# Products with 256 moving tokens: the order of the high and low products over two column blocks, four k-tiles and two PSUM banks

## The chip, the cores and the metric

The kernel runs on one core of a Trainium2 chip. The time is that of one execution on the device, in microseconds (us); shown are the median of three runs and one profiled execution.

## The reference

Two transformer-like blocks are applied to one sequence of 256 tokens with 2048 channels, all in float32.

```python
def reference(x, c, ctx, ...):
    x = first_block(x, c, ctx, ...)      # 2 layers: adaLN, attention + pooling + Fourier branches, gate, w_out
    return second_block(x, ...)          # 1 layer: gated spatial mixing + LRU, w_out, then an FFN

# first_block, per layer: h is the normed, scaled and shifted x
q, k, v, up, uf, g = split_proj(h @ w_in[l])
out = (mixed * jax.nn.silu(g)) @ w_out[l]
...
# second_block
p = jnp.einsum('bsd,de->bse', h, w_in[l])
x = x + jnp.einsum('bse,ed->bsd', y, w_out[l])
up = jnp.einsum('bsd,df->bsf', h, ffn_w_up[l])
x = x + jnp.einsum('bsf,fd->bsd', jax.nn.gelu(gate) * val, ffn_w_down[l])
```

Nearly all of the arithmetic is in these matrix products. In layer 0 of the first block they run over the 256 tokens and 256 context tokens together, from layer 1 on over the 256 tokens alone.

## The kernel before, in words

**Three products for one.** TensorE multiplies in a reduced float32 form (fp32r), so each operand is split in a high part (rounded) and a low part (the rest). A product of weights W and activations H is made of three: W high x H high, W high x H low, W low x H high, all summed in PSUM. A weight chunk (512 KB) is loaded into one of 8 raw buffers (RAW), split by ACT (line 1603, high part) and DVE (line 1847, low part) into one of 4 split buffers (SPL), and multiplied. The activations of a stage lie in HS as 16 k-tiles, each with its high and its low part.

**Forms of product.** A chunk is multiplied by a step of kind "mm" in the function `tensor`. Four forms matter here:

- "tm" groups (lines 1357 to 1359): tokens are stationary, 512 weight columns move; three products of 512 columns for each k-tile, each bank for two k-tiles at a time.
- "wide" groups of layer 0 (lines 1389 to 1391): weights are stationary, 512 tokens move; three products of 512 columns for each k-tile.
- products for one source (lines 1384 to 1386): weights are stationary, 256 tokens move; three products of 256 columns for each k-tile, all three into the same half of one bank.
- "plain" groups (lines 1370 and 1373), which the change touches: weights are stationary, and the high and low parts of the 256 tokens lie side by side, so one product of 512 columns with the high weights makes two of the three (W high x H high into the first half of the bank, W high x H low into the second). The third, W low x H high, is a product of 256 columns; it is added to the second half.

Later the two halves are added anyway (`join`, `x_add`), so it doesn't matter for the sum into which half a low product goes.

**A plain chunk** has 4 k-tiles (512 rows of W) and 256 output columns, two blocks j of 128, each with a bank of its own. A group is four chunks, kc = 0 to 3, which fill the same two banks over 16 k-tiles; the next group takes the next pair of banks. Before, the loop over k-tiles is outside: for each k-tile the high product of block 0, that of block 1, the low product of block 0, that of block 1. These four products are called a quad below; a chunk has four quads. There are 84 plain groups: 16 in layer 1 of the first block (8 of gates, 8 of w_out), 12 in the second block's w_in, 8 in its w_out, 48 in its FFN up product.

**What sets the order.** A planner in Python writes one list of steps (`order`); every engine walks through it and picks its own. Between chunks the planner puts small steps of other work (`hi`, `low`). Each engine takes its steps strictly in turn. A product waits for its weights (`s_lo`), for its bank to be read out (`after`), and, in the first group of a stage, for each k-tile of activations when it comes to that k-tile (`s["inputs"][k]`); the helper `new` leaves out waits that are already known to be met. The last product of a chunk signals `s_chunk`, which frees the split buffer and, after the fourth chunk, the two banks for reading.

**Tiles made on demand.** In the second block's w_out stage ("out2"), tiles 0 to 7 come from the gated mixing branch and 8 to 15 from the LRU branch. Each is made by DVE (line 2088), ACT (line 1749, high part) and POOL (line 2384, low part, kind "y2"). In layer 1's w_out stage the last step of a tile is line 2027 on DVE, in the FFN up stage line 2076 on DVE.

Of the kernel before, what the change touches and what calls it, by code (L numbers as in the profile page):

```python
# [13 lines left out]
KT = 16  # L14
# [45 lines left out]
def two_block_program(nc, I, out):  # L60
    es = ExitStack()
    with es:
# [19 lines left out]
        PS = [es.enter_context(nc.psum_tensor(f"ps{b}", [P, 512], F32)) for b in range(8)]  # L82
# [1199 lines left out]
        for t in range(2):  # L1282
            for kc in range(4):
                run_ahead()
                ks = range(2 * (4 + kc), 2 * (4 + kc) + 2)
# [28 lines left out]
        def tensor(e):  # L1314
            new = Fresh()
            mm, turn = nc.tensor.matmul, nc.tensor.transpose
# [5 lines left out]
            for s in order:  # L1322
                kind, n = s["kind"], s["n"]
# [4 lines left out]
                if kind == "mm":  # L1328
                    i, c = s["i"], s["c"]
                    g, kc = c.group, c.kc  # L1330
                    if g.form == "ada":
# [3 lines left out]
                        for kk in range(2):  # L1335
                            k, q = 2 * kc + kk, 2 * (kc % 2) + kk
                            m = mm(PS[6][32 * q:32 * q + 32, :], CW[:, 2 * k:2 * k + 32], raw_of(i)[:, kk * 512:(kk + 1) * 512],  # L1337
                                   start=kc < 2, stop=kc >= 6, skip_group_check=True)
                        m.then_inc(s_chunk, 1)
                        continue  # L1340
                    w = SPL[:, (split_no[i] - 1) % NSPL, :, :]
                    e.wait_ge(s_lo, split_no[i])
                    stage, l = (g.stage[0], g.stage[1]) if isinstance(g.stage, tuple) else (g.stage, 1)
                    if g.form == "tm":
                        for j in s["banks"]:
                            b, (src, t) = g.banks[j], g.tokens[j]
                            for kk in range(2):
                                k = 2 * kc + kk
                                for sm, v in new(*s["inputs"][k]):
                                    e.wait_ge(sm, v)  # L1350
                                if stage in ("kv", "in"):
                                    hr, hl = (HX(l, k, src, r)[:, t * 128:(t + 1) * 128] for r in range(2))
                                else:
                                    half = HH[1] if stage == "down" else HH[0]
                                    hr, hl = (half[:, k, r, t * 128:(t + 1) * 128] for r in range(2))
                                wr, wl = (w[:, x, kk * 512:(kk + 1) * 512] for x in range(2))
                                mm(PS[b][:, :], hr, wr, start=k == 0, stop=False, skip_group_check=True)  # L1357
                                mm(PS[b][:, :], hr, wl, start=False, stop=False, skip_group_check=True)  # L1358
                                m = mm(PS[b][:, :], hl, wr, start=False, stop=k == KT - 1, skip_group_check=True)  # L1359
                    else:  # L1360
                        half = HH[0] if stage in ("in", "in2", "up") else HH[1]
                        plain = s["src"] is None and not g.wide
                        for kk in range(4 if plain else 0):
                            k = 4 * kc + kk
                            for sm, v in new(*s["inputs"][k]):
                                e.wait_ge(sm, v)
                            hh = half[:, k, :, :].rearrange("p r n -> p (r n)")
                            for j in s["banks"]:
                                wr = w[:, 0, kk * 256 + j * 128:kk * 256 + (j + 1) * 128]
                                mm(PS[g.banks[j]][:, :], wr, hh, start=k == 0, stop=False, skip_group_check=True)  # L1370
                            for j in s["banks"]:
                                wl = w[:, 1, kk * 256 + j * 128:kk * 256 + (j + 1) * 128]
                                m = mm(PS[g.banks[j]][:, 256:512], wl, hh[:, 0:256], start=False, stop=k == KT - 1, skip_group_check=True)  # L1373
                        for j in ([] if plain else s["banks"]):
                            b = g.banks[j] if s["src"] != 0 else FRONT[j]
                            for kk in range(4):
                                k = 4 * kc + kk
                                wr, wl = (w[:, x, kk * 256 + j * 128:kk * 256 + (j + 1) * 128] for x in range(2))
                                for sm, v in new(*s["inputs"][k]):
                                    e.wait_ge(sm, v)  # L1380
                                if s["src"] is not None:
                                    o = PS[b][:, s["src"] * 256:(s["src"] + 1) * 256]
                                    hr, hl = (HL0[:, k, s["src"], r, :] for r in range(2))
                                    mm(o, wr, hr, start=k == 0, stop=False, skip_group_check=True)
                                    mm(o, wr, hl, start=False, stop=False, skip_group_check=True)
                                    m = mm(o, wl, hr, start=False, stop=k == KT - 1, skip_group_check=True)
                                else:
                                    hr, hl = HL0[:, k, :, 0, :], HL0[:, k, :, 1, :]
                                    mm(PS[b][:, :], wr, hr, start=k == 0, stop=False, skip_group_check=True)  # L1389
                                    mm(PS[b][:, :], wr, hl, start=False, stop=False, skip_group_check=True)  # L1390
                                    m = mm(PS[b][:, :], wl, hr, start=False, stop=k == KT - 1, skip_group_check=True)  # L1391
# [7 lines left out]
                elif kind == "columns":  # L1399
                    e.wait_ge(s_vecs, 16 * n_vecs)  # L1400
                    for i, b in enumerate(s["blocks"]):
                        m = turn(PS[5][:, i * 128:i * 128 + BW[b]], STAGE[b][0:BW[b], :], IDN[0:BW[b], 0:BW[b]])
                    m.then_inc(s_colT, 1)

                elif kind == "turn_x":
                    j = s["j"]
                    for t in range(4):
                        for sm, v in new((s_x[t], 16)):
                            e.wait_ge(sm, v)
                        m = turn(PS[j % 3][:, t * 128:(t + 1) * 128], MX[:, t, j * 128:(j + 1) * 128], IDN[:, :])  # L1410
                    m.then_inc(s_turn, 1)

                elif kind == "rstd_b":
                    e.wait_ge(s_diag, n)
                    for t in range(s["nt"]):
                        o = slice(t * 128, (t + 1) * 128)
                        m = mm(PS[s["bank"]][:, o], ONES[:, :], T(s["slot"])[:, o], start=True, stop=True, skip_group_check=True)
                    m.then_inc(s_rs, 1)

                elif kind == "ada_turn":  # L1420
                    e.wait_ge(s_adaE, n)
                    for b in range(4):
                        o = slice(b * 128, (b + 1) * 128)
                        m = turn(PS[7][:, o], T(s["slot"])[:, o], IDN[:, :])
                    m.then_inc(s_adaT, 1)

                elif kind == "sum_turn":
                    e.wait_ge(*s["sums"])
                    for b in range(4):
                        for v, acc in enumerate(s["acc"]):  # L1430
                            m = mm(PS[7][:, 2 * b + v:2 * b + v + 1], acc[:, b * 128:(b + 1) * 128], ONES[:, 0:1], start=True, stop=True, skip_group_check=True)
                    m.then_inc(s_accT, 1)

                elif kind == "n2":
                    e.wait_ge(s_n8, n)
                    for h in range(s["nh"]):
                        o = slice(h * 128, (h + 1) * 128)
                        m = turn(PS[s["bank"]][:, o], lay[s["l"]].QS[:, s["i"], o], IDN[:, :])
# [9 lines left out]
                elif kind == "u2":  # L1448
                    nk = 512 if s["s"] == 0 else 256
                    e.wait_ge(s_pn, n)  # L1450
                    for i in range(nk // 128):
                        o = slice(i * 128, (i + 1) * 128)
                        m = turn(PS[5][:, o], lay[s["l"]].PB[(n - 1) % 2][:, o], IDN[:, :])
# [30 lines left out]
                elif kind == "f1":  # L1484
# [3 lines left out]
                    for src in range(lv.nsrc):  # L1488
                        for t in range(2):
                            m = mm(PS[5][:, src * 256:(src + 1) * 256], lv.QS[:, 2 * src + t, gi * 128:(gi + 1) * 128], lv.CS[:, t, :],  # L1490
                                   start=t == 0, stop=t == 1, skip_group_check=True)
# [983 lines left out]
```

## Time and profile before

| what | value |
|---|---|
| median of three runs | 2326.73 us (2325.6 to 2327.0) |
| profiled execution, its own time | 2325.57 us |
| its span, first to last instruction | 2323.7 us |
| TensorE products (PE) | 2242.7 us busy, x11739 |
| weight loads (PEld) | 1833.1 us busy |
| DVE | 1415.3 us busy |
| ACT | 1039.2 us busy |
| POOL | 273.1 us busy |
| mean granted TensorE clock | 0.988 |

Busy time of an engine is the union of its instructions. A product's duration holds its way through the array, so that products overlap; how fast they follow each other is read from their starts. The 1.9 us between the span and the execution's own time lie outside the instructions.

### The profile page before, as it was taken

The page shows a single profiled execution, that of the slowest core. Times are in us where ns is not written, and L with a number is a line of the kernel's source. Part 1 is how long each engine was busy: PE and PEld are TensorE (multiplying, and loading weights), DVE is VectorE, ACT ScalarE, POOL GpSimd, SP SyncE. Part 2 cuts the span into 40 slices and gives each one's busy share as a digit, 9 for nine tenths or more (in the row PEclk, how much of TensorE's full clock was granted, in tenths as well). Part 3 has the DMA queues.
Part 4 walks back from the last instruction along what each step waited for, and adds up shares of the span by engine and source line. Part 5 has one row for each costly group of instructions (what it writes and reads, how often), then busy time and mean ns, then how long its engine had stood idle before and what let it go on. Part 6 is the DMA issues. An engine that isn't in the chain of part 4 may idle for free.

```text
span 2323.7 us, 30004 instructions
## 1 busy us (share of the span) xinstructions
PE 2242.7 (97%) x11739; PEld 1833.1 (79%) x11739; DVE 1415.3 (61%) x2216; ACT 1039.2 (45%) x1590; POOL 273.1 (12%) x326
## 2 busy tenths in 40 slices
PE   5899999999999999999999998999999999999998
PEld 2477777788788767678888887888888888888887
DVE  3354523477688365546777777677765777567764
ACT  2233333431322254445554565555544555355553
POOL 1011100000011122100021325111100111001111
PEclk8999999999999999999999999999999999999999
DMA  9974433356555475635566544666656665666653
GB/s 358 346 270 150 151 127 115 133 170 206 198 189 175 162 263 190 218 94 169 181 209 195 178 140 154 191 194 186 189 193 190 190 190 185 198 188 190 190 191 117
DMA packets 322428, 437.14 MB, mean 188 GB/s; under 512 B 13848, under 2 KB 220112, under 8 KB 321264
## 3 DMA queue, kind: packets, MB, share of 16 engines
q1 hardware_dynamic: 316800, 413.19, 54.9%
q0 software_dynamic: 3392, 16.90, 2.0%
q10 hardware_dynamic: 2096, 5.15, 0.6%
q8 instruction: 93, 1.52, 0.3%
q14 instruction: 47, 0.39, 0.0%
HBM read 428.89 MB, written 6.29 MB: 187 GB/s over the span
## 4 chain that ended last, share of the span: by engine, by line
PE 87%; DVE 5%; ACT 3%; DMA 2%; issue 2%; POOL 1%; SPq 0%; ACTq 0%; POOLq 0%; DVEq 0%
PE ps L1370 25%; PE ps L1373 12%; PE ps L1357 9%; PE ps L1359 9%; PE ps L1358 9%; PE ps L1389 5%; PE ps L1391 5%; PE ps L1390 5%; PE ps L1337 2%; DVE SPL L1847 2%; ACT SPL L1603 2%; PE ps L1446 1%; PE ps L1463 1%; DMA RAW<-in_w_in_dram 1%; DMA RAW<-in_ada_w_dram 1%
## 5 line engine op out<-in xcount | busy, mean ns | idle before, releaser
L1847 DVE TENSOR_TENSOR SPL<-RAW,SPL 128x1024 fp32r<-128x1024 f32 x592 | 749.2, 1268 | 532.3 <-ACT SPL L1603 530.1
L1370 PE MATMUL ps<-HS,SPL 128*128 128x512 f32 x2688 | 853.6, 399 | 10.2 <-DVE SPL L1847 8.4
L1603 ACT ACTIVATE SPL<-RAW 128x1024 fp32r<-128x1024 f32 x592 | 622.2, 1056 | 477.4 <-PE ps L1359 171.0
L1373 PEld LDWEIGHTS ps<-HS,SPL 128*128 128x128 f32 x2688 | 506.6, 188 | 119.9
L1373 PE MATMUL ps<-HS,SPL 128*128 128x256 f32 x2688 | 529.5, 278 | 0.0
L1370 PEld LDWEIGHTS ps<-HS,SPL 128*128 128x128 f32 x2688 | 412.1, 189 | 15.9 <-issue 7.2
L1357 PE MATMUL ps<-SPL,HS 128*128 128x512 f32 x960 | 396.3, 413 | 11.8 <-DVE SPL L1847 5.3
L1359 PE MATMUL ps<-SPL,HS 128*128 128x512 f32 x960 | 376.8, 393 | 0.0
L1358 PE MATMUL ps<-SPL,HS 128*128 128x512 f32 x960 | 376.5, 392 | 0.0
L1357 PEld LDWEIGHTS ps<-SPL,HS 128*128 128x128 f32 x960 | 181.9, 189 | 74.7 <-issue 17.7
L1358 PEld LDWEIGHTS ps<-SPL,HS 128*128 128x128 f32 x960 | 182.1, 190 | 41.5 <-issue 6.3
L1359 PEld LDWEIGHTS ps<-SPL,HS 128*128 128x128 f32 x960 | 181.7, 189 | 39.5
L1389 PE MATMUL ps<-HS,SPL 128*128 128x512 f32 x480 | 192.8, 402 | 2.7 <-DVE HS L2032 2.7
L1391 PE MATMUL ps<-HS,SPL 128*128 128x512 f32 x480 | 187.7, 391 | 0.0
L1390 PE MATMUL ps<-HS,SPL 128*128 128x512 f32 x480 | 187.4, 390 | 0.0
L2379 POOL TENSOR_TENSOR MM<-MM,GX 128x256 f32<-128x256 f32 x96 | 60.3, 649 | 645.3 <-DVE MM L2013 645.3
L1389 PEld LDWEIGHTS ps<-HS,SPL 128*128 128x128 f32 x480 | 90.5, 189 | 22.6 <-issue 3.7
L1391 PEld LDWEIGHTS ps<-HS,SPL 128*128 128x128 f32 x480 | 90.5, 188 | 19.4
L1390 PEld LDWEIGHTS ps<-HS,SPL 128*128 128x128 f32 x480 | 90.6, 189 | 19.2 <-issue 1.0
L2372 POOL TENSOR_TENSOR TMP<-TMP 128x256 f32<-128x256 f32 (+1 forms) x53 | 56.9, 1073 | 407.8 <-ACT TMP L1738 405.5
L1337 PE MATMUL ps<-RAW,CW 128*32 128x512 f32 x576 | 84.7, 635 | 12.0 <-DMA RAW<-in_ada_w_dram 10.1
L1738 ACT ACTIVATE TMP<-XT 128x256 f32<-128x256 f32 (+1 forms) x58 | 26.8, 468 | 148.8 <-DVE XT L2044 119.6
(291 smaller groups left out, 1839.9 us busy)
## 6 DMA issues: line engine op xcount, KB each, us to landing
RAW<-in_w_in_dram SPq DMA_DIRECT2D x208, 512.0 KB, 5.0
RAW<-in_ada_w_dram SPq DMA_DIRECT2D x192, 512.0 KB, 4.9
RAW<-in_ffn_w_up_dram SPq DMA_DIRECT2D x192, 512.0 KB, 3.6
RAW<-in_w_out_dram SPq DMA_DIRECT2D x96, 512.0 KB, 4.5
RAW<-in_ffn_w_down_dram SPq DMA_DIRECT2D x96, 512.0 KB, 4.1
x_spill<-XT POOLq DMA_DIRECT2D x2, 2048.0 KB, 14.2
XT<-x_spill POOLq DMA_DIRECT2D x1, 4096.0 KB, 13.0
MM<-in_x_dram ACTq DMA_DIRECT2D x2, 1024.0 KB, 10.9
```

The costliest lines, as they stand in the source:

```text
L1337: m = mm(PS[6][32 * q:32 * q + 32, :], CW[:, 2 * k:2 * k + 32], raw_of(i)[:, kk * 512:(kk + 1) * 512], start=kc < 2, stop=kc >= 6, skip_gr ...
L1357: mm(PS[b][:, :], hr, wr, start=k == 0, stop=False, skip_group_check=True)
L1358: mm(PS[b][:, :], hr, wl, start=False, stop=False, skip_group_check=True)
L1359: m = mm(PS[b][:, :], hl, wr, start=False, stop=k == KT - 1, skip_group_check=True)
L1370: mm(PS[g.banks[j]][:, :], wr, hh, start=k == 0, stop=False, skip_group_check=True)
L1373: m = mm(PS[g.banks[j]][:, 256:512], wl, hh[:, 0:256], start=False, stop=k == KT - 1, skip_group_check=True)
L1389: mm(PS[b][:, :], wr, hr, start=k == 0, stop=False, skip_group_check=True)
L1390: mm(PS[b][:, :], wr, hl, start=False, stop=False, skip_group_check=True)
L1391: m = mm(PS[b][:, :], wl, hr, start=False, stop=k == KT - 1, skip_group_check=True)
L1603: act(SPL[:, (n - 1) % NSPL, 0, :], raw_of(i), ACT.Copy).then_inc(s_hi, 1)
L1847: tt(w[:, 1, :], raw_of(s["i"]), w[:, 0, :].bitcast(F32), ALU.subtract).then_inc(s_lo, 1)
L2379: tt(o, o, RSB, ALU.mult).then_inc(s_js, 1)
```

## The change

The nest of the plain products is turned round. Block j is now the outermost loop; inside it go two pairs of k-tiles. For one pair, all into the bank of block j: the high product of the first k-tile, the high product of the second, the low product of the first into the first half of the bank, the low product of the second into the second half. The waits for the activations of a k-tile stand ahead of its high product, as before. Number, shapes and operands of the products stay; only the half of the bank in which the low products of even k-tiles end up is another.

```diff
-                        for kk in range(4 if plain else 0):
-                            k = 4 * kc + kk
-                            for sm, v in new(*s["inputs"][k]):
-                                e.wait_ge(sm, v)
-                            hh = half[:, k, :, :].rearrange("p r n -> p (r n)")
-                            for j in s["banks"]:
-                                wr = w[:, 0, kk * 256 + j * 128:kk * 256 + (j + 1) * 128]
-                                mm(PS[g.banks[j]][:, :], wr, hh, start=k == 0, stop=False, skip_group_check=True)
-                            for j in s["banks"]:
-                                wl = w[:, 1, kk * 256 + j * 128:kk * 256 + (j + 1) * 128]
-                                m = mm(PS[g.banks[j]][:, 256:512], wl, hh[:, 0:256], start=False, stop=k == KT - 1, skip_group_check=True)
+                        for j in s["banks"] if plain else []:
+                            o = PS[g.banks[j]]
+                            for kk in (0, 2):
+                                ks = 4 * kc + kk, 4 * kc + kk + 1
+                                hs = [half[:, k, :, :].rearrange("p r n -> p (r n)") for k in ks]
+                                ws = [w[:, :, (kk + i) * 256 + j * 128:(kk + i) * 256 + (j + 1) * 128] for i in range(2)]
+                                for i, k in enumerate(ks):
+                                    for sm, v in new(*s["inputs"][k]):
+                                        e.wait_ge(sm, v)
+                                    mm(o[:, :], ws[i][:, 0, :], hs[i], start=k == 0, stop=False, skip_group_check=True)
+                                for i, k in enumerate(ks):
+                                    m = mm(o[:, i * 256:(i + 1) * 256], ws[i][:, 1, :], hs[i][:, 0:256], start=False, stop=k >= KT - 2, skip_group_check=True)
```

In the lists of TensorE's instructions below, ps0 and ps1 are the banks of blocks 0 and 1, a product of 128x512 is a high one and one of 128x256 a low one, and x2 stands for two rows alike. Lines 1370 and 1373 are now lines 1372 and 1374.

The first place is where an FFN up group begins, behind the last token-stationary product of the stage ahead of it. Before:

```order
L1359 MATMUL ps3<-SPL,HS 128x512
L1370 MATMUL ps0<-HS,SPL 128x512 [waits split_lo,x_written]
L1370 MATMUL ps1<-HS,SPL 128x512
L1373 MATMUL ps0<-HS,SPL 128x256
L1373 MATMUL ps1<-HS,SPL 128x256
L1370 MATMUL ps0<-HS,SPL 128x512
L1370 MATMUL ps1<-HS,SPL 128x512
L1373 MATMUL ps0<-HS,SPL 128x256
L1373 MATMUL ps1<-HS,SPL 128x256
```

With the change:

```order
L1359 MATMUL ps3<-SPL,HS 128x512
L1372 MATMUL ps0<-HS,SPL 128x512 [waits split_lo,x_written]
L1372 MATMUL ps0<-HS,SPL 128x512
L1374 MATMUL ps0<-HS,SPL 128x256 x2
L1372 MATMUL ps0<-HS,SPL 128x512 x2
L1374 MATMUL ps0<-HS,SPL 128x256 x2
L1372 MATMUL ps1<-HS,SPL 128x512 x2
L1374 MATMUL ps1<-HS,SPL 128x256 x2
```

The sizes follow each other as before, 512, 512, 256, 256; the bank alternated with every product and now changes once a chunk.

The second place is the chunk of the second block's w_out stage with k-tiles 12 to 15 in its first group, where each k-tile is waited for (y_lo is POOL's semaphore of line 2384). Before:

```order
L1370 MATMUL ps0<-HS,SPL 128x512 [waits y_lo,split_lo]
L1370 MATMUL ps1<-HS,SPL 128x512
L1373 MATMUL ps0<-HS,SPL 128x256
L1373 MATMUL ps1<-HS,SPL 128x256
L1370 MATMUL ps0<-HS,SPL 128x512 [waits y_lo]
L1370 MATMUL ps1<-HS,SPL 128x512
L1373 MATMUL ps0<-HS,SPL 128x256
L1373 MATMUL ps1<-HS,SPL 128x256
L1370 MATMUL ps0<-HS,SPL 128x512 [waits y_lo]
```

With the change:

```order
L1372 MATMUL ps0<-HS,SPL 128x512 [waits y_lo,split_lo]
L1372 MATMUL ps0<-HS,SPL 128x512 [waits y_lo]
L1374 MATMUL ps0<-HS,SPL 128x256 x2
L1372 MATMUL ps0<-HS,SPL 128x512 [waits y_lo] x2
L1374 MATMUL ps0<-HS,SPL 128x256 x2
L1372 MATMUL ps1<-HS,SPL 128x512 x2
L1374 MATMUL ps1<-HS,SPL 128x256 x2
```

All four k-tiles are now waited for in the first half of the chunk; the eight products of the second block stand behind the last wait. The instructions of DVE, ACT, POOL and SP keep their order.

## Rows read from the trace of the kernel before

**Rows 1.** The page: span, busy shares, and granted clock in 40 slices.
```profile
span 2323.7 us, 30004 instructions
PE 2242.7 (97%) x11739; PEld 1833.1 (79%) x11739; DVE 1415.3 (61%) x2216; ACT 1039.2 (45%) x1590; POOL 273.1 (12%) x326
...
PEclk8999999999999999999999999999999999999999
```

**Rows 2.** The page: chain of work that ended last, by engine and line.
```profile
PE ps L1370 25%; PE ps L1373 12%; PE ps L1357 9%; PE ps L1359 9%; PE ps L1358 9%; PE ps L1389 5%; PE ps L1391 5%; PE ps L1390 5%; PE ps L1337 2%; DVE SPL L1847 2%; ACT SPL L1603 2%; PE ps L1446 1%; PE ps L1463 1%; DMA RAW<-in_w_in_dram 1%; DMA RAW<-in_ada_w_dram 1%
```

**Rows 3.** Groups by line: busy, mean ns | idle before, releaser.
```profile
L1370 PE MATMUL ps<-HS,SPL 128*128 128x512 f32 x2688 | 853.6, 399 | 10.2 <-DVE SPL L1847 8.4 <-POOL HS L2384 1.6
L1373 PE MATMUL ps<-HS,SPL 128*128 128x256 f32 x2688 | 529.5, 278 | 0.0
```

**Rows 4.** One line, 1583.5 to 1698.3 us: count, min/median/max ns, first and last start.
```profile
L1370 PE MATMUL ps<-HS,SPL x328: 389/396/477, 1583.8 to 1697.7; 128*128 128x512 f32 x164
```

**Rows 5.** The same of line 1357, 1965 to 2049 us.
```profile
L1357 PE MATMUL ps<-SPL,HS x124: 389/389/389, 1964.9 to 2048.5; 128*128 128x512 f32 x124
```

**Rows 6.** Timeline of TensorE, 776.5 to 781.2 us (start us, us, engine, line).
```profile
779.03 0.29 PE L1384 MATMUL ps<-HS,SPL 128*128 128x256 f32 x1
...
781.18 0.28 PE L1384 MATMUL ps<-HS,SPL 128*128 128x256 f32 x1
```

**Rows 7.** Timeline of TensorE, 1784.4 to 1787.3 us: an up group begins.
```profile
1785.18 0.62 PE L1370 MATMUL ps<-HS,SPL 128*128 128x512 f32 x2
1785.63 0.40 PE L1373 MATMUL ps<-HS,SPL 128*128 128x256 f32 x2
1785.86 0.63 PE L1370 MATMUL ps<-HS,SPL 128*128 128x512 f32 x2
1786.33 0.39 PE L1373 MATMUL ps<-HS,SPL 128*128 128x256 f32 x2
1786.56 0.63 PE L1370 MATMUL ps<-HS,SPL 128*128 128x512 f32 x2
```

**Rows 8.** Timeline of TensorE, 1697.3 to 1699.6 us: the last low products, then line 1357.
```profile
1698.13 0.40 PE L1357 MATMUL ps<-SPL,HS 128*128 128x512 f32 x1
...
1698.82 0.39 PE L1357 MATMUL ps<-SPL,HS 128*128 128x512 f32 x1
```

**Rows 9.** Timelines of TensorE in the w_out stage, k-tiles 8 to 15 of group one.
```profile
1438.44 0.63 PE L1370 MATMUL ps<-HS,SPL 128*128 128x512 f32 x2
...
1441.53 0.70 PE L1370 MATMUL ps<-HS,SPL 128*128 128x512 f32 x2
...
1443.11 0.74 PE L1370 MATMUL ps<-HS,SPL 128*128 128x512 f32 x2 [0.63 <-POOL HS L2384]
...
1446.16 0.73 PE L1370 MATMUL ps<-HS,SPL 128*128 128x512 f32 x2 [1.01 <-POOL HS L2384]
1446.73 0.40 PE L1373 MATMUL ps<-HS,SPL 128*128 128x256 f32 x2
1446.96 0.62 PE L1370 MATMUL ps<-HS,SPL 128*128 128x512 f32 x2
```

**Rows 10.** Timelines of POOL there: the low parts of tiles 11, 13 and 15.
```profile
1438.96 0.75 POOL L2384 TENSOR_TENSOR HS<-TMP,HS 128x256 fp32r<-128x256 f32 x1
...
1441.36 1.70 POOL L2384 TENSOR_TENSOR HS<-TMP,HS 128x256 fp32r<-128x256 f32 x1
...
1444.65 1.46 POOL L2384 TENSOR_TENSOR HS<-TMP,HS 128x256 fp32r<-128x256 f32 x1 [0.51 <-ACT HS L1749]
```

**Rows 11.** Timelines: layer 1's w_out, tiles 6 and 7, and chunk of tiles 4 to 7.
```profile
1121.02 0.76 DVE L2027 TENSOR_TENSOR HS<-MM,HS 128x256 fp32r<-128x256 f32 x2
...
1121.37 0.63 PE L1370 MATMUL ps<-HS,SPL 128*128 128x512 f32 x2
```

**Rows 12.** Timelines: the up stage's last tile and the chunk that reads it.
```profile
1521.91 0.48 DVE L2076 SCALAR_TENSOR_TENSOR HS<-XT,VV,HS 128x256 fp32r<-128x256 f32 x1
...
1523.01 0.70 PE L1370 MATMUL ps<-HS,SPL 128*128 128x512 f32 x2
```

## The prediction

> **What bounds the kernel now.** I first read the page. TensorE has products under way for 97% of the span and the granted clock stands at nine tenths or more from the second slice on [rows 1]; the reader is to see that nothing but TensorE's pace can move this time much. The chain that ended last agrees: the two plain lines alone, 1370 and 1373, hold 25% and 12% of it, the splits of DVE and ACT 2% each [rows 2]. The groups by line say how many plain products there are, 2688 high and 2688 low ones, that is 1344 quads, and that TensorE stood idle ahead of them for 10.2 us only [rows 3]. Of these 8.4 us are waits for split weights, which stand at the start of a chunk and don't move with the change, and 1.6 us are waits for POOL's tiles, which do.
>
> Busy times don't tell the pace, since products overlap. So I took starts. In the long undisturbed stretch of the FFN up stage the high products of 164 quads start from 1583.8 to 1697.7 us [rows 4]. The last start is that of a second high product, 0.23 us behind its quad's first; (113.9 - 0.23) / 163 = 0.697 us for a quad.
>
> **The change part by part.**
>
> *What is the same.* 2688 products of 512 columns and 2688 of 256, with as many weight loads, in the same rhythm of sizes (512, 512, 256, 256). The chunk's signal stays on its last product, so split buffers and banks come free at the same point of a chunk. The instructions of the other engines keep their order. These cost nothing, and no cover is needed for that.
>
> *What is new: the bank stays, instead of alternating with each product.* Whether that is worth anything is the question of this change, since 1 ns on a quad is 1.34 us on the kernel. The trace has three other rhythms to compare with:
>
> - Line 1357 to 1359, 512 columns three times into one bank per k-tile: 124 starts of line 1357 from 1964.9 to 2048.5 us are 123 spacings of three products, 83.6 / 369 = 0.2266 us each [rows 5]. Its bank changes only after six products.
> - Lines 1384 to 1386, 256 columns again and again into the same half of one bank: 18 spacings from 779.03 to 781.18 us, 0.119 us each [rows 6].
> - A quad made of these would take 2 x 0.2266 + 2 x 0.119 = 0.692 us, 5 ns under the 0.697 of now.
>
> So at first sight staying in one bank could be worth 5 ns a quad. But two places speak against the bank as the reason. When an up group begins behind line 1359, its first quad, with banks alternating already, goes from 1785.18 to 1785.86 us: 0.68 us. Its two high products take 0.45 us (1785.18 to 1785.63), the same as two of line 1357. The second quad takes 0.70 us and its high products 0.47 us (1785.86 to 1786.33) [rows 7]. The alternation is the same in both; new in the second are the two low products ahead. And behind the last low products of a group, three products of lines 1357 to 1359, in one bank, take 0.69 us (1698.13 to 1698.82) [rows 8] against 3 x 0.2266 = 0.680 in the steady stretch. So high products lose some 6 ns each when they follow short ones, in whichever bank. My reading is that the next weight load just fits under a 256-column product and runs over a little, and the next high products pay for it. The change leaves the sizes in that sequence. I take 0 for the pace.
>
> Both ends for this unknown price: the best that rows allow is every quad like the first one, 2 x 0.2266 + 0.23 (two low products, 1785.63 to 1785.86) = 0.683 us, -14 ns, times 1344 = -19 us. The worst is that low products which stay in one bank fall to the spacing of rows 6 (0.119 instead of 0.115) while high ones keep their 0.47: 0.47 + 0.238 = 0.708, and with the unrounded 0.467 (0.697 less 0.23) 0.705; +8 to +9 ns, +11 to +12 us.
>
> The Trainium skill (TensorE: Matmul & The Clock Gate, section "Back-to-back issue gap") gives N / 2.4 + 2.5 ns as the spacing of warm products, whichever bank they write. By that a quad would take 2 x 215.8 + 2 x 109.2 = 650 ns, 47 ns less than here; were the alternation of banks what keeps this kernel from it, the change would be worth 63 us and the time would be about 2264 us, an estimate from that page. The trace doesn't bear it out, since products that stay in one bank already run at 226.6 and 119 ns.
>
> *What is moved: the waits for tiles.* k-tile 1 of a chunk is now wanted 0.23 us after the chunk's start (before 0.70), k-tile 2 at 0.70 (before 1.39), k-tile 3 at 0.93 us (before 2.09). This matters only in the first group of a stage, and ten products of the chunk now follow the first high product of its fourth tile, where three did. I went through the stages in turn.
>
> - Layer 1's w_out: tiles 6 and 7 are done at 1121.78 at the latest, the chunk of tiles 4 to 7 starts at 1121.37 [rows 11]. Tile 7 is wanted at 1122.30. Tile 6 is the earlier of the two instructions, done about 1121.4, and wanted at 1122.06. No wait; cover of 0.5 us is left.
> - FFN up: the last tile is done at 1522.39, its chunk starts at 1523.01 [rows 12]. No wait; the other tiles are older.
> - Second block's w_out, tiles 8 to 11: the chunk starts at 1438.44 [rows 9]; POOL ends tile 11 at 1439.71 [rows 10], and it is now wanted at 1438.44 + 0.93 = 1439.37. Wait 0.34 plus some 0.06 of hand-over: 0.4 us. Before it was wanted at 1440.5 and there was no wait.
> - Tiles 12 to 15: this chunk started at 1441.53; without waits ahead it is ready at 1438.44 + 4 x 0.697 + 0.4 = 1441.63. Tile 13 comes at 1443.06 and tile 15 at 1446.11 [rows 10] in both versions, since what makes them (ACT, DVE and POOL) doesn't wait for products of this group other than through the split buffers. Tile 15's high product starts at 1446.16 either way. Before, a high and two low products followed, and the next chunk started at 1446.96 [rows 9]. Now what follows is the rest of this high product (0.33, as 1446.16 to 1446.73 is 0.57 for two), two low products (0.23) and block 1's two quads (1.39): 1448.11. That is +1.15 us.
>
> The first loss is swallowed by the second wait, so the sum is +1.15 us, call it +1.2. TensorE is the bound behind this place, so nothing gives it back. Queued behind the wait are only TensorE's own products. Bounds: 0 if the tiles should come sooner, and +3 us if layer 1's w_out also waited for its tiles at the end of each of its two chunks (1.4 us at most for one).
>
> **Sum.** Pace 0, waits +1.2 us: 2325.57 + 1.2 = 2326.8 us for the profiled execution. The median of the runs shown is 1.2 us above that execution, so I forecast 2326.73 + 1.2 = 2327.9 us.
>
> **The rivals.** About 0.2%, 4.7 us, is what a measurement of this kernel can tell from no change.
>
> - *Small gain.* The steady spacings of one-bank rhythms hold, a quad takes 0.692 us: -5 ns, -6.7 us, with the waits 2321 us. For it: rows 5 and 6 are one-bank rhythms and add up to less than rows 4. Against it: they are also rhythms of one size, and rows 7 and 8 show that it is the change of size that costs.
> - *Large gain.* The alternation is what makes the second quad of rows 7 slow (it could need a quad to build up). Then each quad is like the first, -19 + 1.2, 2309 us. Against it: rows 8, where high products in one bank are just as slow behind low ones.
> - *Slower.* Low products into one bank are spaced by 0.119 us instead of 0.115, as in rows 6, and the high ones stay at 0.467: +11 us and the waits, 2339 us. The place is the pair of low products at the end of each quad; it decides when the two halves of one bank are no better for the array than one half. Above 3 ns a quad it shows. For it: rows 6 is the only case of low-sized products in one bank and it is slower. Against it: there a long stream of short products has no long ones among it, and the weight load alone could set that spacing.
> - That the change doesn't do what it says can be left out: the instruction list shows it, row by row.
>
> **How the numbers follow.** No effect on the pace 0.62, 2324 to 2331 us (waits of 0 to 3 us and a nanosecond either way on a quad); small gain 0.10, large gain 0.12; slower 0.16. The range takes in the forecast and both gains and leaves out most of the slower case: 2309 to 2332 us. Faster by over 0.2%: 0.22; within 0.2%: 0.62; slower: 0.16.
>
> **What would show it.** Right: over the stretch of rows 4 the high products of 164 quads again span 113.9 us, with highs in pairs 0.47 us and lows 0.23 us apart; in the w_out stage a wait for POOL ahead of tile 11, and eight products (1.4 us) between tile 15's low product and the next chunk. Behind the first k-tiles of other stages no new waits. Wrong: a quad of 0.69 us or less, or of 0.705 or more, in the undisturbed stretches; or a wait for tiles in layer 1's w_out or in the up stage; or lines 1357 and 1384 with another spacing than before, which would mean that something beside the change moved.

## The result, and the profile after

The changed kernel takes 2332.05 us (median of 22 runs, 2329.69 to 2338.83), the kernel before on the same chips 2328.94 us (22 runs, 2324.94 to 2334.52). The ratio is 1.0017, with a 95% interval of 1.0011 to 1.0022: slower by some 4 us by the ratio (the two medians differ by 3.1), more than the uncertainty of this measurement, and just inside the 0.2% that the prediction called no change. The forecast was +1.2 us.

The page of the kernel after, its profiled execution at 2332.11 us (2325.57 before):

```profile
span 2330.3 us, 30004 instructions
...
PE 2247.0 (96%) x11739; PEld 1835.2 (79%) x11739; DVE 1415.2 (61%) x2216; ACT 1038.9 (45%) x1590; POOL 272.7 (12%) x326
...
PEclk9999999999999999999999998999999999999999
...
L1372 PE MATMUL ps<-HS,SPL 128*128 128x512 f32 x2688 | 856.1, 400 | 11.2 <-DVE SPL L1848 8.2
...
L1374 PE MATMUL ps<-HS,SPL 128*128 128x256 f32 x2688 | 530.5, 279 | 0.0
```

Against [rows 1, 3]: as many products and weight loads, TensorE busy 4.3 us longer, and idle for only 1.0 us more ahead of the high products. Busy time that grows with the same work points to the clock, and slice 25 (1398 to 1456 us) now stands at 8, where [rows 1] has 9. The spans themselves differ by 6.6 us, but 2.8 of these lie ahead of the first plain chunk, in code that was not changed; from one execution to the next this part of the kernel varied by 8 us (first plain chunk at 1003.3 to 1011.2 us in the profiles of this study). So the comparison below goes by stretches between two fixed instructions.

**The pace.** The stretch of [rows 4], one line of the kernel after:

```profile
L1372 PE MATMUL ps<-HS,SPL x328: 389/396/477, 1590.3 to 1704.2; 128*128 128x512 f32 x164
```

Again 113.9 us for 164 quads, to the last digit. The high products of the third round of the up product (512 of them) span 177.87 us in both kernels (the row of before stands below, with the rhythm runs). All plain stretches but one agree within 0.02 us.

**The one stretch that differs** runs from the low part of tile 8, which POOL makes, to the next small product of TensorE, 85 us later; both are the same instructions in every version. Before:

```profile
1436.87 0.74 POOL L2384 TENSOR_TENSOR HS<-TMP,HS 128x256 fp32r<-128x256 f32 x1 [4.26 <-ACT HS L1749]
...
1522.20 0.94 PE L1519 MATMUL ps<-ONES,TMP 128*128 128x1 f32 x8
```

After, the same two, and TensorE's timeline in the two chunks that wait for tiles and behind them:

```profile
1439.72 0.74 POOL L2385 TENSOR_TENSOR HS<-TMP,HS 128x256 fp32r<-128x256 f32 x1 [4.26 <-ACT HS L1750]
...
1441.99 0.43 PE L1372 MATMUL ps<-HS,SPL 128*128 128x512 f32 x1
1442.62 0.50 PE L1372 MATMUL ps<-HS,SPL 128*128 128x512 f32 x1 [0.20 <-POOL HS L2385]
...
1445.96 0.50 PE L1372 MATMUL ps<-HS,SPL 128*128 128x512 f32 x1 [0.98 <-POOL HS L2385]
...
1447.03 0.49 PE L1372 MATMUL ps<-HS,SPL 128*128 128x512 f32 x1 [0.34 <-POOL HS L2385]
...
1449.00 0.80 PE L1372 MATMUL ps<-HS,SPL 128*128 128x512 f32 x1 [1.48 <-POOL HS L2385]
1449.60 0.63 PE L1374 MATMUL ps<-HS,SPL 128*128 128x256 f32 x2
1450.03 1.05 PE L1372 MATMUL ps<-HS,SPL 128*128 128x512 f32 x2
1450.88 0.63 PE L1374 MATMUL ps<-HS,SPL 128*128 128x256 f32 x2
...
1454.65 0.39 PE L1374 MATMUL ps<-HS,SPL 128*128 128x256 f32 x2
1454.88 0.63 PE L1372 MATMUL ps<-HS,SPL 128*128 128x512 f32 x2
...
1528.74 0.95 PE L1520 MATMUL ps<-ONES,TMP 128*128 128x1 f32 x8
```

85.33 us before, 89.02 after: +3.7 us, all in this place. Two things are to be seen. The waits stand where they were forecast: tile 11 is late by 0.40 us (1442.62 instead of 1441.99 + 0.23), and behind tile 15's high product stand ten products of the chunk instead of three. But from tile 15 on everything is stretched: a pair of high products takes 0.85 us (1450.03 to 1450.88), not 0.47. The windows of the same trace tell why; the columns are start and end, length, busy time and count of PE, PEld, DVE, ACT and POOL, granted clock, share of DMA time, GB/s:

```profile
1444.00:1448.00 4.00, 2.21 (x10) 1.25 (x8) 2.96 (x4) 1.67 (x3) 3.15 (x4) 0.96 0.70 220
1448.00:1450.00 2.00, 1.00 (x3) 0.90 (x4) 0.37 (x1) 0.00 (x0) 0.95 (x1) 0.50 0.46 136
1450.00:1452.00 2.00, 2.00 (x8) 1.71 (x7) 0.00 (x0) 0.00 (x0) 0.00 (x0) 0.50 0.64 220
1452.00:1454.00 2.00, 2.00 (x8) 1.71 (x8) 1.14 (x3) 0.26 (x1) 0.00 (x0) 0.50 0.00 0
1454.00:1456.00 2.00, 2.00 (x11) 1.72 (x10) 0.53 (x3) 1.63 (x4) 0.74 (x1) 0.87 0.00 0
```

The granted clock is at its lower level (1.2 instead of 2.4 GHz) from about 1447.7 us (0.96 over the first four) to about 1454.5 (0.87 over the last two), 6.8 us. TensorE had work for 2.21 of the 4 us from 1444 on, and the clock falls while it waits for tile 15, 1.3 us before that wait ends. Before, at the same place of the program, it stays at 1.00, though TensorE works for only half of two microseconds there too:

```profile
1441.00:1445.00 4.00, 3.13 (x15) 2.21 (x13) 2.96 (x4) 1.67 (x3) 3.15 (x4) 1.00 0.67 191
1445.00:1447.00 2.00, 0.99 (x7) 0.76 (x6) 0.52 (x1) 0.00 (x0) 1.10 (x1) 1.00 0.53 160
```

### The profile page after: what moved, and what is told of

It is laid out like the page before. It is cut to its first block, busy times and chain, and to the rows that moved or that the text cites. A ratio compares the mean times of both kernels' runs of the same rounds, so it can differ in the third digit from the quotient of the medians.

```text
span 2330.3 us, 30004 instructions
## 1 busy us (share of the span) xinstructions
PE 2247.0 (96%) x11739; PEld 1835.2 (79%) x11739; DVE 1415.2 (61%) x2216; ACT 1038.9 (45%) x1590; POOL 272.7 (12%) x326
## 4 chain that ended last, share of the span: by engine, by line
PE 86%; DVE 5%; ACT 4%; DMA 3%; issue 2%; POOL 1%; SPq 0%; ACTq 0%; POOLq 0%; DVEq 0%
PE ps L1372 24%; PE ps L1374 12%; PE ps L1357 8%; PE ps L1359 8%; PE ps L1358 8%; PE ps L1390 5%; PE ps L1392 5%; PE ps L1391 5%; PE ps L1337 2%; ACT SPL L1604 2%; DVE SPL L1848 2%; PE ps L1447 1%; DMA RAW<-in_w_in_dram 1%; PE ps L1464 1%; DMA RAW<-in_ada_w_dram 1%
```

## The experiments

All ratios are against the kernel before, on the same chip. "Local" is the stretch of 85.33 us above.

### Is it the two waited chunks, and the clock in them?

**e1** keeps the new nest except in chunks 2 and 3 of the first group of out2; **e2** is its mirror image, the two conditions exchanged. The first loop is the old nest, the second the new one:

```diff
+waited = plain and stage == "out2" and kc > 1 and firsts[stage] is g
-for kk in range(4 if plain else 0):
+for kk in range(4 if waited else 0):
...
-for j in s["banks"] if plain else []:
+for j in s["banks"] if plain and not waited else []:
```

> The new nest everywhere but in two chunks of 336: the second block's w_out stage, first group, k-tiles 8 to 15, where each k-tile is waited for, keep the old nest (k-tiles outside, blocks inside). Theory A (all of the loss arises at these two chunks, as waits and as a lower clock behind them): ratio to before 1.000, within 0.0006; the clock granted there stays at 1.00; the 164 quads of the long up stretch still take 113.9 us. Rival B (the loss is spread over the plain chunks, a little pace each, which one trace may not show): ratio stays near 1.0017.

> The kernel before, with the new nest in those two chunks alone. Theory A: ratio 1.0017 (+3.5 to +4 us): 1.15 us of waits and some 2.5 us of half clock behind them. Rival B: ratio 1.000, or at most 1.0005 for the waits.

Measured: e1 2328.43 us, ratio 0.9995 (0.9986 to 1.0003), local 85.34 us (1442.61 to 1527.95). The new nest in 334 of 336 chunks costs and brings nothing. e2: 2332.02 us, ratio 1.0013 (1.0004 to 1.0021), local 88.02 (1443.24 to 1531.26). Two chunks carry the loss: e1's interval leaves at most 0.7 us to all the others. The waits of e2 are those of the kernel after to the hundredth (0.20, 0.98, 0.34, 1.48 us), but the clock is low only from about 1452.4 on:

```profile
1448.00:1452.00 4.00, 1.73 (x8) 0.86 (x6) 2.85 (x4) 1.67 (x3) 3.15 (x3) 1.00 0.80 252
1452.00:1456.00 4.00, 3.47 (x11) 2.99 (x12) 0.00 (x0) 0.00 (x0) 0.47 (x1) 0.57 0.44 145
1456.00:1460.00 4.00, 4.00 (x25) 3.46 (x24) 2.29 (x5) 2.50 (x5) 0.74 (x1) 1.00 0.00 0
```

0.57 over four us are 3.4 us at the lower level, against 6.8 in the kernel after, and the local loss is 2.7 instead of 3.7 us. The same instructions and the same idle spots can thus come with half-clock stretches of two lengths.

**e3** keeps the waits of the changed kernel, and fills those for tiles 13, 14 and 15 with products.

```diff
 for i, k in enumerate(ks):
+    for _ in range({13: 4, 14: 2, 15: 6}.get(k, 0) if waited and j == 0 else 0):
+        mm(o[:, :], w[:, 1, 0:128], half[:, 12, :, :].rearrange("p r n -> p (r n)"), start=False, stop=False, skip_group_check=True)
     for sm, v in new(*s["inputs"][k]):
         e.wait_ge(sm, v)
```

> The changed kernel, with filler products of 512 columns (low weights of the chunk times k-tile 12) ahead of the waits for k-tiles 13, 14 and 15 in block 0: 4, 2 and 6 of them, 0.92, 0.46 and 1.38 us, each less than the wait of 1.1, 0.5 and 1.7 us that stands there. They are added to the output, which this kernel thereby changes. The waits end when they did; only TensorE is no longer idle in them. Theory A (more than half of the loss is the clock): granted clock 1.00 throughout, loss against before falls to +1.2 us, ratio 1.0005. Rival C (the loss is the wait itself and the clock costs nothing more): ratio 1.0017 as with the change.

Measured: 2330.37 us, ratio 1.0009 (1.0001 to 1.0018), local 86.51 us (1439.33 to 1525.84), +1.2. TensorE is busy through the waits and the clock stays:

```profile
1444.00:1448.00 4.00, 3.92 (x19) 2.81 (x18) 2.94 (x4) 1.67 (x3) 3.16 (x3) 1.00 0.82 244
1448.00:1452.00 4.00, 3.90 (x23) 3.07 (x22) 1.16 (x3) 0.28 (x1) 0.57 (x1) 1.00 0.48 153
1452.00:1456.00 4.00, 4.00 (x25) 3.47 (x24) 2.41 (x4) 3.25 (x6) 0.74 (x1) 1.00 0.00 0
```

This splits the 3.7 us of the profile: 1.2 are the waits and what is queued behind them, 2.5 are the clock. It fits the length too: from 1449.0 to 1454.5 us products run at half clock, 5.5 us for work of 2.75. The interval of e3's ratio (0.2 to 4.2 us) would not separate 1.2 from 3.7 us by itself, but the median of e3 lies 1.65 us under that of e2, on the same chip; in e2's profile the clock costs 1.5 us.

The granted clock of this stretch is 1.00 in all nine profiles with the old nest in the two chunks (before, e1, e5 to e11), and in e3. It fell in both profiles that have the new nest there and nothing in its waits.

**e4** looks for the cheapest nest with pairs: pair of k-tiles outside, block inside, in the two waited chunks; the rest has the old nest. Against the new nest, the two loops change places:

```diff
-for j in s["banks"]:
-    for kk in (0, 2):
+for kk, j in [(kk, j) for kk in (0, 2) for j in s["banks"]] if waited else []:
```

> The kernel before, with half of the new nest in the two waited chunks: pairs of k-tiles outside, blocks inside, so that six products stand behind the last tile's first high product in place of three (before) or ten (change). Worked out from the tile times of before: tile 15's wait ends at the same time and the chunk ends 0.46 us later. Theory A: if the clock holds, ratio 1.0002; if it falls as with the change, +2.5 to +3 us, ratio 1.0012. The granted clock from 1446 to 1455 us tells which; a graded loss without a fall of the clock (about half of 4 us) would speak for rival C.

Measured: 2328.64 us, ratio 1.0002 (0.9993 to 1.0011), local 85.81 us (1438.87 to 1524.68), +0.5. The waits for tiles 13 and 15:

```profile
1445.11 0.50 PE L1386 MATMUL ps<-HS,SPL 128*128 128x512 f32 x1 [1.10 <-POOL HS L2399]
...
1448.16 0.50 PE L1386 MATMUL ps<-HS,SPL 128*128 128x512 f32 x1 [1.38 <-POOL HS L2399]
```

The window between and behind them (columns as above):

```profile
1445.00:1449.00 4.00, 2.51 (x13) 1.98 (x14) 1.48 (x2) 1.57 (x3) 2.26 (x3) 1.00 0.66 206
```

Two gaps, 1.10 and 1.38 us, don't bring the clock down here; in the kernel after they were 0.98, 0.34 and 1.48 us. How much idle time it takes, and how spread, these runs don't show.

### What does the order of sizes cost?

The prediction held that high products behind low ones pay some 6 ns for the change of size. Two runs vary how often the size changes (the waited chunks keep the old nest in all that follow). **e5** runs the eight high products of a chunk and then its eight low ones, as in this edit; **e6** runs the low product of a block directly behind its high one, high, low, high, low.

```diff
+for low in (0, 1) if plain and not waited else ():
+    for kk in range(4):
...
+        for j in s["banks"]:
+            wx = w[:, low, kk * 256 + j * 128:kk * 256 + (j + 1) * 128]
```

> The nest of before in the two waited chunks; in the other 334 plain chunks first the eight high products (k-tiles outside, banks alternating), then the eight low ones. Sizes change twice in a chunk in place of eight times. Theory S (the 5 ns that a quad takes above steady rhythms is paid where high products follow low ones): a chunk falls from 2.787 to 2.77 to 2.78 us (8 x 0.2266, about 0.01 for the change of size, 8 x 0.119 less a few ns), -0.01 us on 334 chunks, -2 to -6 us, ratio 0.9975 to 0.999. Rival T (every low product costs the same wherever it stands, since its successor's weight load runs over): chunk 2.787, ratio 1.000.

> As the run before, but the low product stands straight behind the high one of its block (512, 256, 512, 256, one bank for each pair). Sizes change sixteen times in a chunk. Theory S: a chunk takes more than 2.787 us, some 2.79 to 2.83. Rival T: 2.787. If the bank mattered, a low product straight behind a high one into the same half would also show as a longer spacing between the two than the 0.23 us of now.

e5 measured 2330.02 us, ratio 1.0017 (1.0007 to 1.0026). Its chunk is no quicker with one change of size back and forth than with four:

```profile
1799.89 2.00 PE L1389 MATMUL ps<-HS,SPL 128*128 128x512 f32 x8
1801.73 1.12 PE L1387 MATMUL ps<-HS,SPL 128*128 128x256 f32 x8
1802.69 2.00 PE L1389 MATMUL ps<-HS,SPL 128*128 128x512 f32 x8
```

Eight highs take 1.84 us, eight lows 0.96. Before, they take 8 x 0.2335 = 1.87 and 8 x 0.115 = 0.92. The highs gain 0.03 and the lows lose 0.04: a low product behind a high one is quick (0.113 us), in a row they need 0.120. A chunk takes 2.793 us instead of 2.787: theory S had less, rival T the same. That is 2 us over the 334 chunks by the trace, and 2.2 by the medians (2330.02 and 2327.81 us); the ratio says 4 (1.6 to 6), and the difference stays open.

e6 (one run, 2338.29 us) was to take 2.79 to 2.83 us for a chunk by theory S and 2.787 by rival T. It fits neither throughout: one and the same code runs in two rhythms. Here the 512 high products of the up product's third round, first before the change, then in e6, which is slow there:

```profile
L1370 PE MATMUL ps<-HS,SPL x512: 389/396/398, 1785.2 to 1963.0; 128*128 128x512 f32 x171
```

```profile
L1385 PE MATMUL ps<-HS,SPL x512: 389/398/403, 1792.7 to 1973.3; 128*128 128x512 f32 x171
```

180.54 us instead of 177.87, by starts that are not rounded to tenths. But in layer 1 (53 chunks) the same code took 146.99 us where the kernel before takes 147.69. In the quick rhythm a pair of high and low takes 0.3467 us, 2.773 for a chunk; the highs take 0.230 to 0.233 of it. In the slow one a pair takes 0.3533, 2.827 for a chunk, and the highs take 0.241, 0.236 and 0.233 in turn. So the order with the most changes of size is also the quickest that was seen, and theory S falls too.

**e9** (one run, 2334.86 us) and **e10** ask what decides between them. Both use this order, with `rhythm` set per chunk. In e9 chunk 64 is "old", 208 "long", 272 and 144 to 207 "one" (a quad ahead, then alternating), all others "alt"; in e10 a chunk is "alt" directly behind another plain chunk and "old" behind any small step.

```diff
+seq = {"alt": [(x, p) for p in pairs for x in (0, 1)],
+       "old": [(x, p) for kk in range(4) for x in (0, 1) for p in pairs[2 * kk:2 * kk + 2]],
+       "long": [(x, p) for x in (0, 1) for p in pairs],
+       "one": [(x, p) for x in (0, 1) for p in pairs[:2]] + [(x, p) for p in pairs[2:] for x in (0, 1)]}[rhythm]
+for low, (kk, j) in seq if plain and not waited else []:
```

> One look at how the alternating rhythm (high, low, high, low) of the run before gets into its quick form (2.77 us a chunk, high products 0.230 to 0.233 apart from their low ones, every pair 0.347) or its slow one (2.825, every third high product 0.241). As that kernel, but the first chunk behind line 1359 differs: in the second w_in stage one chunk of the old nest, in the second up round one chunk of highs then lows, in the third round one chunk whose first quad is high, high, low, low; and in the first up round every chunk starts with such a quad. If the form is set by how a stretch begins, at least one of the first three runs at 2.77; if it is set by the place or the banks, all stay at 2.825 as they were. The first up round tells whether a quad in each chunk breaks the slow form: 2.77 to 2.79 if so.

> The run before showed that a stretch which begins with one chunk of the old nest goes over into the quick form of the alternating rhythm (2.77 us a chunk) and stays in it. Here every plain chunk that follows anything but a plain chunk has the old nest, and every other plain chunk alternates high and low products; the two waited chunks keep the old nest. Expected: the long stretches of 53 and twice 63 chunks at 2.77 in place of 2.787 us (146.99, 174.6 and 174.6 us in place of 147.69, 175.55 and 175.55), some 0.5 us in the first up round, -3 to -4.5 us in all, ratio 0.998 to 0.9987. If the way in is more delicate than that one look shows, one or both of the later stretches stay at 2.825 and the kernel is 2 to 5 us slower than before.

In e9 the stretch behind an old chunk was quick (2.773 us, where e6 has 2.83), the third round behind a single quad slow (180.5 us for the 512 highs), the second behind a chunk of highs and then lows slow too. The first up round, with a quad ahead of each chunk, kept neither form: 2.775 to 2.818 us a chunk in its undisturbed part, 2.797 in the mean, a little more than the expected 2.77 to 2.79. That made the old chunk the way in. In e10 the second and third round, behind one old chunk, are quick (63 chunks in 174.72 us each, before 175.55), as expected; but layer 1 behind an old chunk is slow (149.81, before 147.69), and so is the first up round. 2328.52 us, ratio 1.0006 (0.9997 to 1.0015): gains and losses cancel. The rule found in e9 doesn't carry to other stretches; what does set the rhythm is open.

**e11** takes the alternating order only where a run had shown the quick rhythm with the same beginning.

```diff
+rhythm = "alt" if nplain[0] < 64 or 208 < nplain[0] < 272 or nplain[0] > 272 else "old"
```

> Old nest in all plain chunks but these, which run high, low, high, low: the first 64 (up to the end of layer 1), and the second and third round of the up product without their first chunk each. Theory Q (the rhythm that a stretch falls into is set by how it begins, and lasts to its end): these three stretches begin as they did in the runs where the quick rhythm was seen, so 53 chunks take 146.99 us (147.69 before) and 63 chunks 174.7 us twice (175.55 before): -0.7 and -1.7, with the first ten chunks some 0.1; -2.4 us in all, ratio 0.9990, and nothing lost elsewhere, where the nest is the old one. Rival D (the way in is more delicate than that, as when the first stretch ran slow behind an old chunk): one or more of the three run at 2.825 us a chunk, which costs 2.1 to 2.5 us each: between 0 and +6 us, ratio 1.000 to 1.0025.

All three stretches came out as expected: 146.99, 174.72 and 174.72 us. The third round:

```profile
L1394 PE MATMUL ps<-HS,SPL x512: 389/395/398, 1790.0 to 1967.1; 128*128 128x512 f32 x171
```

177.1 us, 0.7 under the kernel before. The stretches add up to -2.4 us. The runs say 2326.24 us against 2327.87, ratio 0.9994 (0.9985 to 1.0003): in the direction expected, but not told apart from no change.

### Does it pay to hold the clock elsewhere?

The kernel before has such falls of its own. The longest in its plain groups goes with a wait of 4.8 us for split weights, which ends at 1405.7 us. **e7** is the kernel before with 18 filler products ahead of that wait (they write a bank that the next product starts afresh, so the sum is the same); **e8** is e5 with them.

```diff
+if g is last_in2 and kc == 0:
+    for _ in range(18):
+        mm(PS[g.banks[0]][:, :], HH[0][:, 0, 0, 0:128], HH[0][:, 0, :, :]..., start=True, stop=True, ...)
 e.wait_ge(s_lo, split_no[i])
```

> The kernel before, with 18 filler products of 512 columns (18 x 0.227 = 4.1 us) ahead of the first chunk of the second block's last w_in group, where TensorE waits 4.8 us for split weights and then runs its four quads at half the clock. They go into the group's own bank, which its first product clears, from a tile of activations that lies still, so that the sum is not changed. If the clock falls through idleness alone, it now holds, and the chunk behind the wait takes 2.9 us in place of 5.05: -2.1 us, ratio 0.9991. If it falls anyway, or the fillers run beyond the wait: 1.000 or a little more.

> The two runs together: highs then lows in unwaited chunks, and the fillers. The gains should add: -4 to -8 us by theory S, ratio 0.9965 to 0.998; -2 us by rival T.

e7: 2329.73 us, ratio 1.0007 (0.9999 to 1.0016); e8: 2331.74 us, ratio 1.0015 (1.0005 to 1.0025), no better than e5. The same microseconds of both traces (columns as above), first before the change, then in e7:

```profile
1404.00:1411.00 7.00, 5.27 (x17) 4.53 (x18) 5.46 (x7) 5.30 (x10) 4.56 (x5) 0.54 0.30 94
```

```profile
1404.00:1411.00 7.00, 6.41 (x32) 5.06 (x30) 4.46 (x8) 4.35 (x9) 5.30 (x8) 1.00 0.22 75
```

The clock held, as meant, and nothing came of it. The timeline of e7 shows where the gain went:

```profile
1403.23 4.25 PE L1344 MATMUL ps<-HS 128*128 128x512 f32 x18
1408.08 0.73 PE L1374 MATMUL ps<-HS,SPL 128*128 128x512 f32 x2 [0.59 <-DVE SPL L1851]
...
1411.84 0.74 PE L1374 MATMUL ps<-HS,SPL 128*128 128x512 f32 x2 [0.71 <-DVE SPL L1851]
...
1421.54 0.70 PE L1374 MATMUL ps<-HS,SPL 128*128 128x512 f32 x2 [0.66 <-DVE SPL L1851]
```

From the waited chunk to the fourth behind it e7 takes 13.46 us (1408.08 to 1421.54). Before it is 13.41 (1405.73 to 1419.14). The faster chunk runs into DVE's next splits and waits for them. Here the splits set the pace, not TensorE; behind tile 15 of out2 it is TensorE, and there the clock is paid in full.

## Why the prediction was right, and where it failed

The forecast was 2327.9 us, the measured median 2332.05, 4.2 us more. Of these, 2.2 us are no effect of the change: the kernel before has a median of 2328.94 in the 22 runs beside it, and 2326.73 in the three that the forecast started from. The rest is the change itself, +3.1 us by the medians (+4.0 by the ratio) instead of +1.2. That it still lies within 0.2%, as the prediction thought likeliest, is luck in part: some 2.5 us of it by the profile stand in no term of the sum.

**Pace 0: right.** 113.9 us for 164 quads before and after; e1 adds that 334 chunks with the new nest change nothing. Whether products alternate between banks or stay in one is worth nothing here. So the rivals "small gain", "large gain" and "slower" all fall. The quickest order tried takes 2 x 346.7 = 693 ns for the work of a quad. The estimate of 650 ns that follows from the Trainium skill (TensorE: Matmul & The Clock Gate, section "Back-to-back issue gap") is reached by none. The section calls its formula that of the isolated gap, with no budget for the weight load at small sizes. The prediction left this out; here every product has a weight load of its own (x11739 of both), so the estimate was no fair rival.

**The reading beneath it: only half right.** That bank is not what separates the first quad of [rows 7] from the second was right. That each change of size costs the highs 6 ns was not: e5 has a quarter of the changes and is not quicker, and e6, with twice as many, is in its quick rhythm quicker than all. What highs gain in a row, lows lose in a row, and all orders tried end between 2.773 and 2.827 us for a chunk. Why, these runs don't show; the reading that a weight load runs over was not tested. The forecast rested on the sizes keeping their sequence, which the change does leave alone, and so the flaw did no harm.

**The waits: right, place by place.** No wait in layer 1's w_out and none in the up stage; tile 11 late by 0.40 us (forecast 0.4); tiles 13 and 15 waited for. +1.2 us forecast, +1.2 in e3, where the waits stand alone. By the same sum e4's nest has one high and two low products more behind tile 15 than the old one, 0.46 us; measured 0.48.

**The step that failed is the last of the waits:** "Queued behind the wait are only TensorE's own products", and a Sum of pace and waits alone. TensorE's products were priced at the full clock. The new waits made four idle spots out of two, 3.0 us in all instead of 1.6, and thinned the work between them to 2.21 of 4 us; the clock fell, and the products queued behind the last wait, the very ones that the change had put there, ran at half pace until 1454.5 us. That is the missing +2.5 us (+1.5 in e2). That a wait can have this price was to be read before: the kernel's own trace has half-clock stretches at waits, with pairs of high products that last 1.2 us instead of 0.63:

```profile
1393.59 1.22 PE L1370 MATMUL ps<-HS,SPL 128*128 128x512 f32 x2 [2.55 <-DVE SPL L1847]
...
1405.73 1.19 PE L1370 MATMUL ps<-HS,SPL 128*128 128x512 f32 x2 [4.82 <-DVE SPL L1847]
```

Both waits are far longer than the new ones, so that trace could give the price but not foretell the fall. The bound of +3 us for the waits came from another mechanism (waits in layer 1's w_out) and was not enough; the measured 2332.05 us lie 0.05 above the end of the range.

The Trainium skill (TensorE: Matmul & The Clock Gate, section "A second HAM failure mode: psum-queue depth-cycling") tells of a kernel that idles shortly but often and whose clock goes back and forth. The trace agrees in so far as the clock fell here with no single gap over 1.5 us; it did so once and came back.

## What to carry to other kernels

When an edit gathers waits of the bounding engine more closely, or puts more of its products behind one, price those products at both levels of the clock: look in the trace for stretches as thin as the new one will be, and read there whether the clock fell. A nest over tiles that arrive one by one should keep the tile outermost, so that little is left behind the last wait; where the tiles are there already, the nest was free. And before holding a clock with fillers, ask who is the bound behind the wait: by the profiles it saved 2.5 us at one place of this kernel and nothing at another.

## What was not expected of the hardware

- Around the same products and the same idle spots (0.20, 0.98, 0.34, 1.48 us) the clock was low for 6.8 us in one execution and 3.4 us in another, which makes 1 us of difference in the time.
- One order of products, high and low in turn, has two steady rhythms, 2.773 and 2.827 us for a chunk. Each lasted for a whole stretch of 53 or 63 chunks without changing over, in which nothing else differed; other products ahead of a stretch switched it from one to the other, but by no rule that held in all of them.
